# The mixing's output product as three f32r products

## The reference, cut to what matters

```python
# x: 1024 prompt rows and 8 x 16 sample rows, D_MODEL = 1024; h is x, outs the three head groups
merged = jnp.concatenate([rms_norm(og.reshape(b, t, -1)) for og in outs], axis=-1)
merged = (merged * g_mix_out).astype(h.dtype)
h = h + merged @ w_out                       # the product that is changed: 1152 x 1024 x 1024
y = hier_moe(rms_norm(h, norm_ffn).reshape(b * t, D_MODEL), ...)   # routing, then 16 experts
h = h + y
gate = jax.nn.sigmoid(rms_norm(h, norm_ple) @ w_ple_gate)
return h + (p_i @ w_ple) * gate
```

## Time and profile before

| | |
|---|---|
| time, median of 3 runs | 1398.94 us (1398.64 to 1399.96) |
| the profiled execution | 1400.65 us, of which the span of instructions is 1399.0 us |
| TensorE matmuls busy in the span | 1270.9 us (91%) |
| TensorE weight loads | 915.4 us (65%) |
| VectorE, ScalarE, GpSimd busy | 547.9, 454.4, 137.6 us |
| L1258, the output product of the mixing | 288 records, 65.7 + 63.3 us |
| L408, the projection's f32r products | 1296 records |

### The profile page before, as it was taken

The page is one execution under the profiler, slowest core; times in us unless marked ns, Lnnn a source line. Parts: engine busy times, 40 slices in busy tenths (PEclk is TensorE's granted clock), DMA queues, the critical chain, the costliest instruction groups (busy, mean ns, idle before and its releaser), DMA issues. The chain is left out here.

```text
span 1399.0 us, 18860 instructions
## 1 busy us (share of the span) xinstructions
PE 1270.9 (91%) x7192; PEld 915.4 (65%) x7192; DVE 547.9 (39%) x993; ACT 454.4 (32%) x993; POOL 137.6 (10%) x204
## 2 busy tenths in 40 slices
PE   4899999999789999987879999559999999999997
PEld 3677878888556666655554555357887778746776
DVE  4634564300245455687842222452122221213343
ACT  4523222211255555566643332311111111013321
POOL 6110000000000000000034000040111111002110
PEclk9899999999899999999989999669999999999999
DMA  7433344314536466534289841077888898643331
GB/s 261 159 99 92 123 151 125 113 49 149 211 97 217 151 208 182 175 112 142 55 267 246 255 139 45 15 237 239 254 237 242 247 264 245 215 125 116 119 107 45
DMA packets 100060, 228.38 MB, mean 163 GB/s; under 512 B 22809, under 2 KB 50468, under 8 KB 93839
## 3 DMA queue, kind: packets, MB, share of 16 engines
q1 hardware_dynamic: 77487, 161.26, 35.6%
q0 software_dynamic: 16160, 53.50, 13.4%
q10 hardware_dynamic: 6336, 12.58, 3.1%
HBM read 171.55 MB, written 57.71 MB: 164 GB/s over the span
## 5 line engine op out<-in xcount | busy, mean ns | idle before, releaser
L408 PE MATMUL zp<-w_low,x_high 128*128 128x512 f32 x432 | 176.6, 409 | 18.9 <-DVE w_low L532 17.1
L1638 PE MATMUL moe_gu<-moe_xT,moe_room 128*128 128x208 f32 x1024 | 187.4, 341 | 0.6 <-ACT moe_xT L1738 0.6
L1638 PEld LDWEIGHTS moe_gu<-moe_xT,moe_room 128*128 128x128 f32 x1024 | 181.2, 192 | 8.5 <-issue 7.5
L408 PE MATMUL zp<-w_high,x_low 128*128 128x512 f32 x432 | 172.7, 400 | 0.0
L408 PE MATMUL zp<-w_high,x_high 128*128 128x512 f32 x432 | 172.4, 399 | 0.0
L937 PE MATMUL heads_turn<-ident,heads_prob 128*128 128x128 f32 x626 | 94.4, 285 | 24.3 <-ACT heads_probT L1009 24.3
L1649 PE MATMUL moe_yp<-moe_room,moe_hid 128*104 128x512 f32 x256 | 112.6, 592 | 2.0 <-DVE moe_hid L1820 2.0
L408 PEld LDWEIGHTS zp<-w_low,x_high 128*128 128x128 f32 x432 | 82.6, 191 | 38.4 <-issue 17.1
L1825 DVE COPY moe_y<-moe_yp 104x512 f32<-104x512 f32 x64 | 44.3, 692 | 154.8 <-PE moe_yp L1649 154.8
L1009 ACT ACTIVATE heads_probT<-heads_turn 128x512 f32<-128x512 f32 (+2 forms) x136 | 71.7, 544 | 83.3 <-PE heads_turn L937 83.1
L484 ACT ACTIVATE z<-zp,ssx 128x512 f32<-128x512 f32 x54 | 37.1, 687 | 187.2 <-PE zp L408 186.9
(11 more groups left out here) (283 smaller groups left out, 1735.0 us busy)
## 6 DMA issues: line engine op xcount, KB each, us to landing
moe_room<-in_w_gu SPq DMA_DIRECT2D x16, 2048.0 KB, 14.4
moe_room<-in_w_ed POOLq DMA_DIRECT2D x16, 1024.0 KB, 13.1
scratch_grouped<-mix_zeros POOLq DMA_DIRECT2D x32, 416.0 KB, 23.7
scratch_grouped<-moe_y SPq DMA_DIRECT2D x16, 832.0 KB
h<-in_w_in ACTq DMA_DIRECT2D x12, 1024.0 KB, 6.4
scratch_qkT<-ring SPq DMA_DIRECT2D x36, 256.0 KB, 2.3
heads_ckT<-in_cache_kT SPq DMA_DIRECT2D x9, 1024.0 KB, 5.2
heads_cv<-in_cache_v SPq DMA_DIRECT2D x9, 1024.0 KB, 4.9
```

Source lines behind the costliest of these rows:

```text
L408: mm = pe.matmul(zp[:, U % 3, :], xs[:, k, n * P:n * P + P], ws[g % 2][:, k, :], start=(k == 0 and i == 0), stop=(k == KD - 1 and i == 2))
L1638: mm = pe.matmul(gu[:, u, side, BS * f:BS * f + BS], wgu[u][:, k, DE * side + P * f:DE * side + P * f + P], xT[u][:, k, :], start=(k == 0 ...
```

## The change

The upper part and the rest of the weights are made as the stage begins: `split` on ScalarE (8 copies of 128x512 for each half of the columns), `lower_weights` on VectorE (8 subtractions for each half). The rests `w_low` lie where the loaded `w_out` lies and take its place. The rows' upper part is the copy out of PSUM, now into an f32r `mT`; VectorE subtracts it from the same PSUM rows (`lower`). mix does three f32r matmuls where it did one float32 one. `sq` and `zeros` use memory of the blocks before. In `moe`, ScalarE waits for the stored x rows ahead of the gate's split, since the memory of `xn` is used again.

```diff
+        w_high = [sb(f"w_high{i}", [P, KD, 512], F32R) for i in two]
-        mT = [sb(f"mT{u}", [P, KD, P]) for u in two]
+        mT = [sb(f"mT{u}", [P, KD, P], F32R) for u in two]
+        mT_low = [sb(f"mT_low{u}", [P, KD, P], F32R) for u in two]
-        sq = sb("sq", [P, D])
+        sq = mixw["spare"][:, 0:D]
-        zeros = sb("zeros", [ROWS, D // 4])
+        zeros = mixw["spare"][0:ROWS, D:D + D // 4]
...
-                    turn(lambda j: m2[:, P * j:P * j + P], tm, m_normed, m_copied, n, m_turned)
+                    turn(lambda j: m2[:, P * j:P * j + P], tm, m_normed, m_lowered, n, m_turned)
...
                     for half in two:
-                        pe.wait_ge(m_copied, 2 * n + 2)
+                        pe.wait_ge(m_lowered, 2 * n + 2)
                         wait(pe, h_ready, n)
                         for k in range(KD):
-                            mm = pe.matmul(om[:, half, :], mT[n % 2][:, k, :], w_out[half][:, k, :],
-                                           start=(k == 0), stop=(k == KD - 1))
+                            if n == 0:
+                                pe.wait_ge(w_lowered, KD * half + k + 1)
+                            for i, (ms, ws) in enumerate(((mT, w_low), (mT_low, w_high), (mT, w_high))):
+                                mm = pe.matmul(om[:, half, :], ms[n % 2][:, k, :], ws[half][:, k, :],
+                                               start=(k == 0 and i == 0), stop=(k == KD - 1 and i == 2))
...
+                def split(i):
+                    for k in range(KD):
+                        act.activation(w_high[i][:, k, :], w_out[i][:, k, :], ACT.Copy).then_inc(w_split, 1)
+
                 group_scale(0)
+                split(0)
                 copies(tm, mT[0], m_turned, mixed, 0, 0, m_copied)
+                split(1)
...
+                def lower_weights(i):
+                    for k in range(KD):
+                        dve.wait_ge(w_split, KD * i + k + 1)
+                        dve.tensor_tensor(w_low[i][:, k, :], w_out[i][:, k, :], w_high[i][:, k, :].bitcast(F32), ALU.subtract)\
+                           .then_inc(w_lowered, 1)
+
+                def lower(n):
+                    for half in two:
+                        dve.wait_ge(m_copied, 2 * n + half + 1)
+                        wait(dve, mixed, n - 1)
+                        hi = mT[n % 2][:, 4 * half:4 * half + 4, :].rearrange("p j n -> p (j n)")
+                        lo = mT_low[n % 2][:, 4 * half:4 * half + 4, :].rearrange("p j n -> p (j n)")
+                        dve.tensor_tensor(lo, tm[:, half, :], hi.bitcast(F32), ALU.subtract).then_inc(m_lowered, 1)
+
                 norm_heads(0)
+                lower_weights(0)
+                lower(0)
+                lower_weights(1)
...
                         residual(n)
+                    if n + 1 < NT:
+                        lower(n + 1)
                     if n > 0:
                         take_logits(n - 1)
...
                 act.wait_ge(gate_loaded, 16 * 3)
+                for u in two:
+                    act.wait_ge(x_stored[u], 16 * ((NT + 1 - u) // 2))
```

More of the change, by code:

```diff
@@ L1181, in mixing @@
         two = range(2)
-        w_out, w_r, b_r, gmo, gff, gcol = (mixw[n] for n in ("w_out", "w_r", "b_r", "gmo", "gff", "gcol"))
+        w_out, w_low, w_r, b_r, gmo, gff, gcol = (mixw[n] for n in ("w_out", "w_low", "w_r", "b_r", "gmo", "gff", "gcol"))
+        w_high = [sb(f"w_high{i}", [P, KD, 512], F32R) for i in two]
         xr = sb("xr", [P, 2, D])
@@ L1204, in mixing @@
         m_copied = sem("m_copied")
+        m_lowered = sem("m_lowered")
+        w_split = sem("w_split")
+        w_lowered = sem("w_lowered")
         mixed = sem("mixed")
@@ L1986, in program @@
             sbb = lambda n, s, d=F32: both.enter_context(nc.sbuf_tensor(n, s, d))
-            past1, wide = sbb("past1", [P, KD * 512]), sbb("w_out1", [P, KD, 512])
+            with nc.sbuf_tensor("past1", [P, KD * 512], F32) as past1, nc.sbuf_tensor("w_out1", [P, KD, 512], F32) as wide:
+                pass
+            w_low = [sbb(f"w_out_low{i}", [P, KD, 512], F32R) for i in range(2)]
             k1, v1 = sbb("heads_kT1", [P, TOK]), sbb("heads_v1", [P, NT * 2 * HD])
@@ L1992, in program @@
             mixw = {"w_out": [past1[:, :].rearrange("p (k n) -> p k n", k=KD), wide[:, :, :]],
-                    "w_r": sbb("w_router", [P, KD, NG + NE]), "b_r": sbb("b_router", [P, NG + NE]),
-                    "gmo": k1[:, 0:D], "gff": v1[:, 0:D], "gcol": sbb("norm_ffn_cols", [P, KD])}
+                    "w_low": [w[:, :, :] for w in w_low], "w_r": sbb("w_router", [P, KD, NG + NE]), "b_r": sbb("b_router", [P, NG + NE]),
+                    "spare": early["z"], "gmo": k1[:, 0:D], "gff": v1[:, 0:D], "gcol": sbb("norm_ffn_cols", [P, KD])}
             heads(nc, c, a, dram, merged, released, early, late, mixw)
```

## The result

| | before | after |
|---|---|---|
| time, median of 4 runs | 1398.79 us (1398.51 to 1399.96) | 1378.08 us (1377.41 to 1379.62) |
| ratio | | 0.985 (0.9835 to 0.9859) |
| span of the profiled execution | 1399.0 us | 1378.0 us |
| start of norm_heads to the first routing operation | 167.35 us | 147.43 us |

The change makes the kernel 20.7 us faster. The prediction said 16.0 us: 1383 us, with a range from 1379 to 1391. The sign and the mechanism were right, the gain was sized too low.

What follows compares the result with a forecast made beforehand. Mixing was taken to run at TensorE's pace: +3.2 us at mix(1), 8 tiles x -2.53 = -20.2, 7 x 0.15 = +1.05, sum -16.0, so 1383 us from the median of 1398.94; range 1379 to 1391.

Steps and rivals of the forecast that it cites:

- The pace of the product: Mixing's output product: f32r matmuls 0.233 us apart as in the gate, 11.29 us instead of 13.82, 2.53 us less a tile.
- The wait for the rest of mT: Steady tiles: mix waits for VectorE's row subtractions, ready at 816.55 against 816.56; 0.15 us a tile charged, 0 to 0.5 possible.
- The start: First tile: splitting the weights delays mix(0) by 3.6 us, to 733.2, and mix(1) by 3.2 us.
- The slow steps: mix(0): 14 matmuls at the half clock, 0.427 us instead of 0.233, costing 2.7 us; bounds 0 and 14.
- The end of the stage: Last product and last rows up to routing: -2.53 us, from the product alone.
- The rest of the kernel: Everything outside the mixing stage: 0 us, with ScalarE's new wait ahead of the gate's split hidden.
- a shorter start: First tile of the mixing: the start costs less than charged, total 1378 us; chance 0.02.
- B: Rival, gaps between the mixing's products: the clock falls in each of the 8, +24 us, 1407 us; chance 0.05.
- C: Rival, start of the mixing: GpSimd slows VectorE's subtractions, 4.1 us more ahead of mix(0), 1387 us; chance 0.11.
- D: Rival, mixing's product: f32r matmuls don't reach 0.233 us; at 0.26, 11.7 us less gain, 1395 us; chance 0.05.
- E: Rival, after the mixing: a later wait holds the start of the expert blocks, and 1399 us stays; chance 0.02.

Runs made afterwards that it cites:

- mt_shift: Changed kernel with 64 bytes of padding ahead of `mT`, so the transposed rows begin at 96 modulo 256 and the weights stay at 32; 1381.06 us, ratio 0.9874.
- all_shift: Changed kernel with 64 bytes of padding ahead of the weights' rests, so all four operands of the mixing's product move together from 32 to 96; 1378.29 us, one execution.
- place_256: Changed kernel with padding ahead of the projection's x tiles, the gate's rows and its upper weights, so every f32r operand begins at 32 modulo 256; 1370.87 us, ratio 0.9797.
- no_row_rests: Changed kernel without VectorE's subtraction of the rows and its wait, the upper part multiplied twice; 1412.01 us with other routing, so only the mixing is read.
- after_again: The changed kernel, unaltered, run and traced once more in the third series; 1376.59 us, ratio 0.9851.
- one_block_split: Changed kernel splitting only one of 8 weight blocks for each half and using it for all k; 1454.41 us with other routing, so only the mixing is read.
- start_by_product: Changed kernel with mix(0) doing all upper products first, then row rests, then weight rests, and the splitting reordered to suit; 1374.2 us, ratio 0.9825.
- run 432: Not a label of a run: the words count the mixing's f32r matmuls, which are run 432 times in the changed kernel; no time of its own.
- phase_all: Changed kernel with 64 bytes of padding ahead of the projection's `x_high`, the gate's rows and `wg_high`; 1377.53 us, ratio 0.9854.
- moving_shift: Changed kernel with the mixing's upper weights alone moved 64 bytes, to 96, and the rows kept at the same remainder of 256; 1378.68 us, one execution.

## Why the prediction was wrong in size

**The pace of the product (failed, the largest term that every trace shows).** I took 0.233 us from the gate as what an f32r matmul costs, and 2.53 us a tile from it. Here it is 0.227, a product 11.04 us instead of 11.29, 2.78 us less a tile. Over nine tiles that is 9 x 0.25 = 2.2 us. It is shown, not argued: mt_shift brings my pace back with 64 bytes of padding, all_shift and place_256 show that the place of the operands against each other decides. The row was right and the step from it was not: gate and projection both had their operands 64 bytes apart modulo 256, and the mixing's came to lie at one place. Why the place counts, no run here shows.

**The wait for the rest of mT (failed, small).** 7 x 0.15 = 1.05 us charged, nothing measured: the gap is 3.58 us in both kernels, and no_row_rests bounds the wait at 0.05 us a tile. The sum 816.55 against 816.56 was right to the hundredth; I should have taken it at its word, with the charge in the range alone.

**The start (right in kind, 0.5 us too dear in one trace and 2.0 in the other).** mix(0) waits for VectorE's subtraction, as said: +3.37 instead of +3.6 (8 subtractions in 4.90 us, where I had 4.96). mix(1) followed the transposes by 747.26 - 744.52 = 2.74 instead of 2.85. The slow steps are the term that isn't fixed: I charged 14, and there were 14 in the first trace and 7 in after_again, so mix(1) came at +2.72 and at +1.17 instead of +3.2. The nine other kernels with the f32r product have 7 to 13. The 14 that I charged from the kernel's start were one draw, and that they came true in the first trace is luck. one_block_split and start_by_product show that the order of the splitting sets when mix(0) begins.

**The end of the stage (not predicted).** -3.20 instead of -2.53: 0.25 is the pace. The other 0.4 is the moment at which the granted clock fell. Before, it fell within the last 8 transposes (0.80 over 886 to 887), in the changed kernel only 2.2 us after their start (1.00 over 864 to 866, 0.77 over 866 to 867), so they took 1.55 and 1.07 us. In after_again it fell 0.6 us after their start, and all but 0.1 us of this gain is gone; so it is chance too. First the kernel before, then the changed one:

```profile
886.16 1.55 PE L1244 MATMUL mix_tx<-ident,h 128*128 128x128 f32 x8
```

```profile
864.35 1.07 PE L1249 MATMUL mix_tx<-ident,h 128*128 128x128 f32 x8
```

**The rest of the kernel.** -1.1 us in the first pair of traces, -4.1 with after_again, most of it in attention. Nothing was changed there but ScalarE's wait, which is hidden, and the mixing begins anywhere between 720.6 and 725.4 us in the ten traces that have the projection of before; what moves it is open.

For the first trace the terms add up: 16.0 + 2.0 (pace, 8 tiles) + 1.05 + 0.5 + 0.4 = 19.9 us, the measured 19.92, and with the last 1.1 the 21.0 us between the spans. Only the first two, 3.1 us, come again in each trace. The medians are 4.7 us beyond the forecast; the other 1.6 lie in the clock of the start and the end and in the rest of the kernel, and these traces don't divide them further. The mistake of the range was of the same kind: its lower end, 1379, held a shorter start but took the pace as known, because one row showed it well. 0.006 us on a matmul that is run 432 times is 2.6 us, against the 4 us between the forecast and that lower end, which the measured time missed by 0.9. That I had put 1378 beside "a shorter start" is luck: the time came out there, but more through the pace and the wait than through the start.

**The rivals.** B (clock falls between the tiles) fell: 1.00 over 745 to 861. The Trainium skill (TensorE: Matmul & The Clock Gate, "Part 4: PE-mode transpose") says that a transpose doesn't count as busy in the way that a matmul does; here 3.6 us of transposes and of 20-column matmuls between two products cost no clock. C (GpSimd slows VectorE) fell: GpSimd is busy in 8.69 of 9 us while the 8 subtractions take 0.61 us each. D had the right question, whether 0.233 carries over, and the wrong sign: I had asked only for reasons why it should be slower, DMA traffic above all, and traffic did nothing visible to it: the DMA engines are busy 0.92 of the time over 722 to 800 us and 0.32 over 800 to 861, and the products take 11.0 to 11.1 us in both. E fell: the routing starts when the logits are there, and the gate's split waits for nothing new.

## What to carry to other kernels

A duration taken from the same instruction elsewhere in the kernel is a sample with its own conditions, the operands' addresses among them: where it is multiplied by hundreds, leave a few per cent of it in the range on both sides. One trace is also one draw of when the clock becomes full: trace the same kernel twice before a term of 1 or 2 us at a stage's start is explained. When two SBUF operands feed a stream of f32r matmuls, try to let them begin at the same place modulo 256 bytes and look at the distance of the starts. Where an operand is split at the start of a stage, begin with the product that needs the fewest of its parts.

## What the runs showed of the hardware

- f32r matmuls of 128x128 by 128x512 with a weight load each start 0.227 us apart when all operands of the stream begin at the same remainder of 256 bytes (all at 32, all at 96), and 0.2324 to 0.2334 in the mean when some are off: rows 64 bytes behind the weights (mt_shift 0.2333, projection and gate 0.2334), 128 behind (phase_all's projection 0.2325), the weights of two products of three 64 behind the rows (moving_shift 0.2324, 0.231 or 0.233 by tile), or one pair of three 128 apart (phase_all's gate 0.2329). Other distances were not tried. That is up to 2.6%, and 5.7 to 7.2 us of this kernel between the changed kernel and place_256, by which of their medians are compared.
- The time from the first matmul of mix(0) to full speed isn't fixed: the short steps (0.23 us from one start to the next, 0.43 before) begin 6.14 us after it (730.63 to 736.77) in the changed kernel and 3.03 us after it (728.69 to 731.72) in after_again, the same kernel; before both, TensorE had stood idle for 4.05 us. In the other kernels with the f32r product it is between 3.15 and 5.71 us. mix(1) moves with it by 1.55 us in one and the same kernel, more than the 1.38 us by which start_by_product's gain at mix(1) (4.75 us against the first trace) exceeds its gain at mix(0) (3.37).
